# Two decoder layers with routed experts: the eight experts ordered by token count and written out one by one

## The reference

```python
def moe_swiglu(h, w_router, w1, w3, w2):
    logits = (h @ w_router).astype(jnp.float32)
    top_val, top_idx = lax.top_k(logits, TOP_K)
    top_w = jax.nn.softmax(top_val, axis=-1)
    combine = jnp.sum(jax.nn.one_hot(top_idx, N_EXPERTS, dtype=jnp.float32) * top_w[..., None], axis=-2)
    out = jnp.zeros_like(h)
    for e in range(N_EXPERTS):
        out = out + combine[..., e:e + 1].astype(h.dtype) * swiglu(h, w1[e], w3[e], w2[e])
    return out
```

## Time and profile before

| what | value |
|---|---|
| median of three runs | 1893.97 us |
| lowest and highest run | 1892.99 and 1896.91 us |
| the profiled execution, first to last instruction | 1888.4 us |
| busy: PE, DVE, ACT, POOL | 99%, 81%, 65%, 4% |
| experts, from PE's first block of expert 0 to its last | 918.4 to 1877.9 us |
| DMA before the experts and in them | about 180 and about 380 GB/s |

### The profile page before, as it was taken

The page is one execution under the profiler, slowest core; times in us unless marked ns, Lnnn a source line. Parts: engine busy times, 40 slices in busy tenths (PEclk is TensorE's granted clock), DMA queues, the critical chain, the costliest instruction groups (busy, mean ns, idle before and its releaser), DMA issues.

```text
span 1888.4 us, 26841 instructions
## 1 busy us (share of the span) xinstructions
PE 1874.6 (99%) x10585; PEld 1630.8 (86%) x10586; DVE 1537.2 (81%) x1382; ACT 1235.1 (65%) x1110; POOL 80.9 (4%) x85
## 2 busy tenths in 40 slices
PE   9999999999999999999999999999999999999998
PEld 9989998999999998998988888888888888888886
DVE  7999965575568999765788988888888888888886
ACT  5566745454455565654677777777777777777775
POOL 1000000100010000000010001000010010000000
PEclk9999999999999999999999999999999999999999
DMA  9544544355555445553799999999999999999992
GB/s 333 179 172 157 180 169 180 141 180 189 187 167 185 172 154 180 180 199 112 301 370 377 387 389 353 398 375 383 383 352 400 379 381 381 354 408 376 377 398 106
DMA packets 76263, 521.36 MB, mean 276 GB/s; under 512 B 9360, under 2 KB 9616, under 8 KB 14992
## 3 DMA queue, kind: packets, MB, share of 16 engines
q1 hardware_dynamic: 72464, 507.84, 70.6%
q0 software_dynamic: 2992, 11.01, 2.0%
q10 hardware_dynamic: 720, 1.31, 0.3%
HBM read 512.79 MB, written 7.34 MB: 275 GB/s over the span
## 4 chain that ended last, share of the span: by engine, by line
PE 90%; DVE 4%; ACT 3%; issue 1%; DMA 0%; SPq 0%; ACTq 0%; DVEq 0%
PE psum L1702 21%; PE psum L1704 21%; PE psum L1703 21%; PE psum L1716 14%; PE psum L1717 7%; DVE wlo L1055 2%; ACT whi L571 2%; PE psum L2202 1%; PE psum L1970 1%; PE psum L1950 1%; DMA raw<-in_stream 0%; DVE U L1078 0%; PE psum L1868 0%; PE psum L1891 0%; PE psum L1829 0%
## 5 line engine op out<-in xcount | busy, mean ns | idle before, releaser
L1055 DVE TENSOR_TENSOR wlo<-raw,whi 128x2048 fp32r<-128x2048 f32 x477 | 1086.1, 2283 | 251.0 <-ACT whi L571 250.5
L571 ACT ACTIVATE whi<-raw 128x2048 fp32r<-128x2048 f32 x477 | 909.6, 1909 | 245.7 <-PE psum L1704 195.5
L1702 PE MATMUL psum<-whi,act_hl 128*128 128x512 f32 x1408 | 556.2, 395 | 0.8
L1704 PE MATMUL psum<-whi,act_hl 128*128 128x512 f32 x1408 | 549.0, 390 | 0.0
L1703 PE MATMUL psum<-wlo,act_hl 128*128 128x512 f32 x1408 | 548.2, 389 | 0.0
L1716 PE MATMUL psum<-h_hl,whi 128*128 128x512 f32 x1216 | 430.7, 398 | 0.3 <-DVE U L1413 0.2
L1717 PE MATMUL psum<-h_hl,wlo 128*128 128x256 f32 x1216 | 340.5, 280 | 0.0
L1702 PEld LDWEIGHTS psum<-whi,act_hl 128*128 128x128 f32 x1408 | 264.4, 188 | 57.8 <-DVE wlo L1055 4.1
L1704 PEld LDWEIGHTS psum<-whi,act_hl 128*128 128x128 f32 x1408 | 264.2, 188 | 56.1
L1703 PEld LDWEIGHTS psum<-wlo,act_hl 128*128 128x128 f32 x1408 | 264.6, 188 | 53.9 <-issue 0.7
L1716 PEld LDWEIGHTS psum<-h_hl,whi 128*128 128x128 f32 x1216 | 228.2, 188 | 55.3 <-issue 1.1
(11 more groups left out here) (253 smaller groups left out, 1391.8 us busy)
## 6 DMA issues: line engine op xcount, KB each, us to landing
raw<-in_stream SPq DMA_DIRECT2D x474, 1024.0 KB, 6.9
raw<-in_stream SPq DMA_DIRECT2D x6, 512.0 KB, 3.9
U<-in_stream SPq DMA_DIRECT2D x2, 1024.0 KB, 11.1
xacc<-U POOLq DMA_DIRECT2D x3, 512.0 KB, 7.9
xT<-in_x_cols ACTq DMA_DIRECT2D x4, 256.0 KB, 6.7
raw<-in_stream SPq DMA_DIRECT2D x4, 256.0 KB, 7.6
memhat<-in_mem_cols SPq DMA_DIRECT2D x1, 1024.0 KB, 19.6
hrow<-U POOLq DMA_DIRECT2D x1, 1024.0 KB, 6.0
```

The lines of the kernel that those rows point to most:

```text
L571: act.activation(whi[:, n % SPLIT, 0:words], src[:, 0:words], ACT.Copy).then_inc(hi_ready, 1)
L1055: dve.tensor_tensor(wlo[:, n % SPLIT, 0:words], src[:, 0:words], whi[:, n % SPLIT, 0:words].bitcast(F32), ALU.subtract).then_inc(lo_ready, 1)
L1702: pe.matmul(o, st[0], mv[0], start=start, stop=False, **kw)
L1704: return pe.matmul(o, st[1], mv[0], start=False, stop=stop, **kw)
```

## The change

The rule for which expert comes when becomes a value found on the chip: DVE sorts the experts 1 to 7 by their counts (`ranked`) and puts counts, positions, combine weights and the list of experts into that order (`ordered`, `listed`). Expert 0 stays first. All eight experts are written out on SP, ACT, DVE and PE; SP loads the number of the next expert into a register, once for each, and adds it to the address of the load. The three idle areas join the ring: from the experts' first block on, a ring of RING = 9 is used, and a load waits for the split of nine blocks before. The first of them is loaded in the memory attention of layer 1 already. The code has a cheaper form for experts with few tokens, but `few(p)` is False for all, so that each has its three products as before, and no instruction of that form runs.

```diff
+RING = RAW + EXTRAS
+HALF = SLOTS // 2
+def few(p):
+    return False
...
+                    if lay and (what, i) == ("xq", 0):
+                        sp.wait_ge(m_hi_s, 4)
+                        sp.wait_ge(m_lo_s, 4)
+                        fetch(0, RAW)
...
-            def experts(r):
...
-                if r == 0:
-                    expert(0, ahead_of=SPLIT + RAW)
-                    with sp.Fori(1, NE - 1) as e:
-                        expert(e)
-                    expert(NE - 1, PER_E - EXTRAS)
...
+            for p in range(NE):
+                if p == 1:
+                    sp.wait_ge(count_ready, 2)
+                e = sp.value_load(order[0:1, p:p + 1], min_val=0, max_val=NE - 1) if p else 0
+                for c in range(PER_E):
+                    n = MOE + PER_E * p + c
+                    if p or c >= RING:
+                        sp.wait_ge(lo_ready, n - RING + 1)
+                    elif c < RAW:
+                        sp.wait_ge(lo_ready, n - RAW + 1)
+                    elif c == RAW + 1:
+                        sp.wait_ge(ss_done, 6)
+                    elif c == RAW + 2:
+                        sp.wait_ge(ht_done, 4)
+                    if p or c != RAW:
+                        fetch(p, c, e)
```

POOL gets 13 more small instructions (iotas, memsets, three selects on 128 x 128) ahead of its `memset(y)`. On DVE the following is added or moved:

```diff
+            square = [P, NE, NE]
+            def ranked():
+                dve.wait_ge(cnt_done, 2)
+                dve.wait_ge(rt_const, 21)
+                mine(dve.scalar_tensor_tensor(key, bank[7][:, 304:312], float(NE), key_add, op0=ALU.mult, op1=ALU.add))
+                settled()
+                mine(dve.tensor_tensor(prod[:, 0:NE, :], key.unsqueeze(2).to_broadcast(square),
+                                       key.unsqueeze(1).to_broadcast(square), ALU.is_gt))
+                settled()
+                mine(dve.tensor_reduce(rank, prod[:, 0:NE, :], AX.X, ALU.add))
+                settled()
+                mine(dve.tensor_tensor(order_of, rank_at.unsqueeze(2).to_broadcast(square),
+                                       rank.unsqueeze(1).to_broadcast(square), ALU.is_equal))
+                settled()
+            def ordered(to, what):
+                for b, row in enumerate(what):
+                    mine(dve.tensor_tensor(prod[:, NE * b:NE * b + NE, :], order_of, row.unsqueeze(1).to_broadcast(square),
+                                           ALU.mult))
+                settled()
+                for b in range(len(what)):
+                    mine(dve.tensor_reduce(to[b], prod[:, NE * b:NE * b + NE, :], AX.X, ALU.add))
+                settled()
             def counted():
...
-                mine(dve.tensor_reduce(cntf, bank[7][:, 304:312], AX.X, ALU.max))
+                ordered((over,), (bank[7][:, 304:312],))
+                mine(dve.tensor_tensor(over, over, cap, ALU.subtract))
                 settled()
-                dve.tensor_copy(cntu[:], cntf).then_inc(count_ready, 1)
+                mine(dve.tensor_reduce(cntf, over, AX.X, ALU.max))
+                settled()
+                dve.tensor_scalar(cntu[:], cntf, float(SLOTS), None, ALU.add).then_inc(count_ready, 1)
+                ordered(tuple(posp[:, b, :] for b in range(TB)), tuple(posm[:, b, :] for b in range(TB)))
+            def listed():
+                ordered((ordf,), (iota8,))
+                dve.tensor_copy(order[:], ordf).then_inc(count_ready, 1)
...
+                    for c in range(SPLIT, PER_E + SPLIT):
+                        if p == 0 and c == SPLIT + 1:
+                            ranked()
+                        if p == 0 and c == SPLIT + 2:
+                            counted()
+                        if p == 0 and c == SPLIT + 3:
+                            weights()
+                        if p == 0 and c == SPLIT + 4:
+                            listed()
+                            for b in range(TB):
+                                in_slots(slice(1, NE, 2), iota, posp, b)
+                                ins = in_slots(slice(2, NE, 2), iota, posp, b)
+                            ins.then_inc(round_own, 1)
+                        if p == 0 and c == 16:
+                            places()
```

```diff
                 if f == 0:
                     counts()
-                elif f == 1:
+                elif f == 2:
                     indices()
...
-                        if f == 0:
-                            pe.wait_ge(y_ev, e + 8 * r + 1)
+                        if f == 1:
+                            pe.wait_ge(y_ev, p + 1)
```

More of the change, by code:

```diff
@@ new lines, in second_round @@
+            def second_round():
+                first = MOE + NE * PER_E
+                for p in range(NE):
+                    e = sp.value_load(order[0:1, p:p + 1], min_val=0, max_val=NE - 1)
+                    for c in range(PER_E):
+                        sp.wait_ge(lo_ready, first + PER_E * p + c - RAW + 1 if p or c >= RAW else first)
+                        at, _ = again(c)
+                        sp.dma_start(raw[:, at, :], stream[bass.ds(PER_E * e + (MOE + c), 1)].rearrange("a p w -> p (a w)"))\
+                          .then_inc(w_raw[at], 16)
@@ L944, in body, with first_round @@
+            def first_round():
+                gathered(1, 0)
+                act.wait_ge(wts_s, 1)
+                act.activation(wts[:, 2:4], wts[:, 0:2], ACT.Exp).then_inc(re_ready, 1)
+                act.activation(small[:, 35:36], small[:, 32:33], ACT.Silu)
+                for p in range(NE):
+                    n_e, k_e, last = MOE + PER_E * p, FSTEPS * p, p == NE - 1
                     for c in range(SPLIT, PER_E + SPLIT):
-                        if opening and c in (15, 21, 27):
-                            x_rows((c - 9) // 6)
@@ new lines, in first_round @@
+                        if c == PER_E + 2 and not last:
+                            act.wait_ge(w_used, n_e + PER_E)
+                            if few(p):
+                                act.wait_ge(scr_in, 48)
+                            else:
+                                act.wait_ge(wc_ready, p + 1)
+                            for k in range(2):
+                                at = slice(512 * k, 512 * k + 512)
+                                if few(p):
+                                    ins = act.activation(ysum[:, at], bank[4 + k][:], ACT.Copy)
+                                else:
+                                    ins = act.activation(y[:, at], bank[4 + k][:], ACT.Copy, scale=wcur)
+                            ins.then_inc(halves_out if few(p) else y_ev, 1)
@@ new lines, in in_slots, with hidden @@
+            def in_slots(which, numbers, where, b):
+                some = sel[:, b, which, :]
+                shape = [P, len(range(NE)[which]), SLOTS]
+                return dve.tensor_tensor(some, numbers.unsqueeze(1).to_broadcast(shape),
+                                         where[:, b, which].unsqueeze(2).to_broadcast(shape), ALU.is_equal)
+            def hidden(f, count, used):
+                dve.wait_ge(e_silu, count)
+                dve.wait_ge(w_used, used)
+                dve.tensor_tensor(eg, bank[2 * (f % 2) + 1][:], esil[:, f % 2, :], ALU.mult).then_inc(e_g, 1)
@@ new lines, in again_split, with body @@
+                def again_split(e, c):
+                    n0 = first + c
+                    split_at(raw[:, again(c)[0], :], n0, PER_E * e + n0 + 1)
+                for c in range(SPLIT):
+                    again_split(0, c)
+                for k in range(2):
+                    gathered(NE + 1, k, 0)
+                def body(e, last):
+                    k_e = FSTEPS * e + NE * FSTEPS
+                    for c in range(SPLIT, PER_E + SPLIT):
+                        for f in range(FSTEPS):
+                            if f and c == gate_end(f) + SPLIT:
+                                transposed(k_e + f, f - 1, 0)
+                            if c == up_end(f) + SPLIT:
+                                hidden(f, k_e + f + 1, PER_E * e + first + up_end(f) + 1)
+                            if f < 4 and c == up_end(f) + SPLIT + 1:
@@ new lines, in up, with turn @@
+            def up(n0, value, half, o):
+                pe.wait_ge(lo_ready, value)
+                for k in range(4):
+                    tok = tuple(a[:, P * (4 * half + k):P * (4 * half + k) + P] for a in (he_hi, he_lo))
+                    ins = three(o, tok, wt(n0, k, 512, 0, 512), half == 0 and k == 0, half == 1 and k == 3)
+                ins.then_inc(w_used, 1)
+            def turn(k_e, f):
+                pe.wait_ge(e_g, k_e + f + 1)
+                for k in range(4):
+                    ins = pe.transpose(bank[6][:, P * k:P * k + P], eg[:, P * k:P * k + P], ident[:])
+                ins.then_inc(e_tr, 1)
```

716 lines of the change are left out of this document (407 added, 309 removed).

## The result

The changed kernel takes 1896.51 us (median of 20 runs, 1894.21 to 1900.85) beside 1893.90 us for the kernel before (20 runs, 1890.62 to 1896.91). The ratio is 1.0019, with a 95% interval of 1.0013 to 1.0026: slower by 2.5 to 4.9 us, where +5.0 was forecast. That lies just on the line of 0.2% between "slower" and "no change". A second measurement of the same kernel, with the last experiments, gave 1.0017 (1.0008 to 1.0026). Each ratio in this document is to the kernel before, measured beside the kernel in question; the interval is the one of 95%.

What follows compares the result with a forecast made beforehand. PE was taken to bound the kernel, with DVE having the least to spare. Profiled span 1888.4 us + 5.5 (DVE's opening) - 0.5 (loop) = 1893.4, plus 5.6 to the median: 1899.0 us, range 1894.5 to 1902.8.

Steps and rivals of the forecast that it cites:

- DVE's opening: Expert 0, blocks 4 to 7: DVE's added sorting makes PE wait ahead of blocks 5, 6 and 7, 5.5 us in all.
- the pieces: DVE's `ranked`, `counted`, `weights`, and `listed` with the selection, ahead of blocks 4 to 7: together 8.1 us.
- The loop: Writing out the experts removes the loop's 0.08 us of the bubble after each boundary, six times: -0.5 us.
- by that rule: At the six loop-backs, the skill's rule should show stalls of a fetch each; the trace was said to disagree.
- The code stream: Straight code of six more experts, fetched late, would give 1943 us (rival 3, 0.05 with anything as large); argued against.
- The ring: Loads of the experts: nine buffers instead of six remove nothing, as nothing on PE's path waits for a load; cost 0.
- From span to time: Last step of the sum: median of the runs taken as 5.6 us above the profiled span, 1893.4 to 1899.0 us.
- the forecast's own: Whole kernel's time: the range of the forecast without its rivals, 1897 to 1902.4 us, chance 0.62.
- the line to "same": Whole kernel's time: a sum below +3.8 us, 0.2% of the time, counts as no change.
- rival 1: Opening of expert 0: DVE keeps up, not slower, if the pieces take 6.9 us or less; chance 0.27.
- the lead of 2.6 us: Opening of expert 0: DVE's lead over PE, which the added DVE time must exceed to stall PE (8.1 - 5.5).

Runs made afterwards that it cites:

- experiment 6: Changed kernel, nine buffers kept, each load held back until the split of six blocks before: 1.0036; again 1.0028, beside 1.0017 for the unaltered changed kernel.

## Why the prediction was right, point by point

- **DVE's opening.** Right in mechanism, place and order. Block 4 has no gap. The added wait (beyond the usual 0.23 us, with the slower restart) is 1.1 us ahead of block 5 (1.3 forecast), 1.6 ahead of block 6 (1.8), 2.2 ahead of block 7 (2.45), none after: 4.9 us instead of 5.5. The mis-sized term is the pieces: from its first start to the start behind it, `ranked` took 0.96 us (0.97 forecast), `counted` 1.74 (1.95), `weights` 2.05 (2.17), `listed` and the selection 2.73 (3.0); 7.5 instead of 8.1. A 128x64 operation does take 0.21 to 0.23 us, but two independent ones take 0.35 together, which the earlier trace rows hinted at with their cheaper pairs. (The parts that I named for `weights` add up to 2.10, not 2.17.)
- **The clock.** Missing from the sum. The gap of 2.1 us brought 1.6 us at the lower clock behind it in the profiled execution, so the opening cost 6.5 there, not 5.5. It isn't there each time: of the five profiles with these three gaps, three have the fall behind the third (in the changed kernel's second profile with another behind `indices`), and the two with the loads held back have one behind `indices` only.
- **The loop.** Right in size too. The bubble shrank from 0.52 to 0.45 or 0.44 us, and the distance from one expert to the next, over six of them, from 118.94 to 118.86 us: -0.5 us in all, as forecast. In the times, the kernels with straight code and no sorting stand at 0.9991 and 0.9985, their counterparts with the loop at 1 and 0.9990: agreeing with -0.5 us, and not fine enough to show it. That there is nothing large to win at the loop-backs, as the earlier trace rows said, is borne out: with the branches gone, no more than 0.09 us each came back. The Trainium skill (Runtime: NRT & Kernel Launch, Instruction fetch mechanics) has a fetch at a taken branch only where the target is out of the current two pages of instructions. My "by that rule" skipped that condition; no run here shows whether the loop's first instruction was out of them, so the small size doesn't speak against the rule.
- **The code stream.** The straight code's 80 packets delayed nothing; steps of the written-out experts take 16.8 us as before.
- **The ring.** Took no wait from ACT, DVE or PE; its cost of 0 is not contradicted, but experiment 6 leaves 0.1% of the time open.
- **From span to time.** This step was wrong. I added 5.6 us, the distance of the profiled span of 1888.4 us to the median. In all 20 executions of the changed kernel the time lies 1.7 to 1.85 us above the span of the same execution. The profiled execution of the kernel before was therefore one of about 1890.2 us, below the lowest of its 20 runs, and the typical one, it seems, contains stretches at the lower clock already. That fits profiles that differ by 5.3 us (1893.7 - 1888.4), medians by 2.6 and a ratio that gives 3.6. With 1.8 in place of 5.6 the same sum gives 1895.2 us; the profiled execution took 1895.41. The forecast of +5.0 came close to the profiles' difference by luck: the missing clock (+1.6) was nearly made up for by the oversized pieces (-0.6) and by 0.7 us by which the changed kernel happened to reach the experts earlier.
- **The chances.** The median of 1896.51 us lies in the whole range (1894.5 to 1902.8), but just below the forecast's own (1897 to 1902.4), and the loss, 2.6 us by the medians or 3.6 by the ratio, stays under the 3.8 that I gave as the line to "same". By the time alone that is rival 1's outcome, to which I gave 0.27. Its mechanism isn't: the gaps are there, and the pieces took 7.5 us, not the 6.9 or less that it needed (and not my 8.1). Less the lead of 2.6 us and the loop's 0.5, they give +4.4. So the mechanism was right on its merits; that the time fell into the range in spite of a wrong step to the median was helped by the range's width.

## What to carry to other kernels

Where one engine prepares blocks for another through a ring of three, work put ahead of one block costs the consumer its full length minus the small lead (here 7.5 - 4.9 = 2.6 us), however idle the engine is on average; look for a stretch in which the preparing engine itself waits (here 4.14 us), and put the work there. The price of a gap on TensorE is the gap plus what the clock does behind it, which differs from one execution to the next. Before comparing a profile with a median, compare it with the time of its own execution.

## What the runs showed of the hardware

- TensorE's granted clock fell to one half for some 3 to 6 us of work around three kinds of stretch: behind a gap of 2.1 us that followed gaps of 1.0 and 1.6 (in three of five profiles), at a gap of 4.4 us after the same two (one profile), and, without any wait before it, at 32 matmuls of 10 columns in one piece of 3.5 us. The last is seen at the piece or behind it in seven of the ten profiles that have it whole. With the 32 in four pieces of 0.95 us between blocks the clock stayed at 1.00 in that place in all four profiles.
- The fall isn't the same in each execution of one program: the changed kernel's first profile had one in this half, its second had three, one of them ahead of the experts. That one is in 3 of 14 profiles and cost 2.8 us each time. The mean granted clock of an execution, 0.999 to 0.994, goes with most of the scatter of 6 to 9 us between executions. What decides whether it falls in a given execution stays open.
